# First attention: scores kept with turned sign, small norms spread between the index units, and GpSimd or VectorE scaling probabilities in place of ScalarE

## The chip, the cores and the metric

One core of a Trainium2 chip runs the whole program. The time is the device time of one execution in microseconds, lower is better; a comparison uses the median of several executions. TensorE (PE) does the matmuls and transposes, VectorE (DVE) and ScalarE (ACT) the elementwise work, GpSimd (POOL) helps with elementwise work, and SyncE (SP) issues the DMAs. Each engine runs its own instruction list in order and waits on semaphores that the others raise.

## What is computed

Two transformer blocks over 512 tokens of width 1024, all in float32. The change touches only the attention of the first block, in which two kinds of heads share one stage:

```python
def dsa_sparse_attention(q, k, v, q_idx, k_idx, w_idx):      # 8 heads, one shared key and value head
    top_k = min(TOPK_MAX, T // 4)                            # 128 of 512 keys
    def one_block(i):                                        # 128 queries
        idx_logits = jnp.einsum('bqhd,bsd->bqhs', qib, k_idx)        # 16 index heads of 64
        score = jnp.einsum('bqh,bqhs->bqs', wb, jax.nn.relu(idx_logits))
        score = jnp.where(causal[None], score, -jnp.inf)
        _, sel = lax.top_k(score, top_k)
        ...
        att = jnp.einsum('bqhd,bqkd->bqhk', qb, kg) * scale  # masked where not valid
        p = jax.nn.softmax(att, axis=-1)
        return jnp.einsum('bqhk,bqkd->bqhd', p, vg)

def mla_attention(c_q, c_kv, k_rope, g_q_lat, g_kv_lat, w_uq, w_ukv, cos_b, sin_b):   # 8 causal heads
    q = (rmsnorm(c_q, g_q_lat) @ w_uq)...                    # the small norms: 384 and 256 features
    kv = (rmsnorm(c_kv, g_kv_lat) @ w_ukv)...
    ...
        p = jax.nn.softmax(s, axis=-1)
        return jnp.einsum('bhqs,bshd->bqhd', p, v)
```

## The kernel before

The order of all work is written out by hand, engine by engine; semaphores tie the engines together. A feed-forward stage comes first, then the projections of the first block, and then the three parts that matter here.

**Index stage.** `INDEX` lists 48 index units, 16 index heads times three query tiles (query tile 0 needs no selection). For each unit PE multiplies (L874, banks 0 to 3 in turn), ACT takes the Relu into one of three slots of `SF` (L1290), and DVE adds it with its weight to the score tile in `BIAS` (L1717). The three slots mean that ACT can be at most three units ahead of DVE, and four PSUM banks that PE can be at most four ahead of ACT. Ahead of the units DVE applies the two small norms, `norm_q` in three pieces of 128x512 and `norm_kv` in two: `norm_scaled` (L1480) scales a piece into `VA`, ACT copies it rounded into `NH` (`norm_high`, L1166), and `norm_low` (L1492) keeps the rest in `NL`. The factor that they multiply by is spread over the partitions by PE (L640), after index unit 2 for `norm_q` and after unit 3 for `norm_kv`. Then DVE splits one weight tile (`split`, L1456, into `WL`), and only then takes unit 0. Units 24 to 31 of PE's list carry the values' matmuls (`values`, L843 to L845). GpSimd copies `KPE` into `KB` (L2032) as soon as the small norms are done.

**Heads.** `UNITS` lists 64 units of 128 queries: 32 of the causal heads (head by head, query tiles 0 to 3, so 128, 256, 384 and 512 keys in turn) and 32 of the sparse heads (query tile by query tile, 8 heads each). `project` (twice, ahead of units 0 and 16) makes queries and keys of four causal heads. A unit u passes through

1. PE `scores` (L929) into bank u % 2;
2. DVE `masked` (L1763): scale, add the mask, write to slot u % 4 (`VA` or, every fourth, `SA`) and take the row maximum into `NM`;
3. DVE `negated` (L1770): turn the sign of `NM`, raise `at_m`;
4. ACT `exp` (L1320) with the sum of the row into `DEN`;
5. DVE `inverse` (L1774);
6. ACT `normalised` (L1327): scale the probabilities in their slot;
7. PE `turn` (L936): one to four transposes into bank 2 + u % 2;
8. ACT `turned` (L1335): copy them to `PT`.

Each engine's loop runs over u with the steps three, two or one units ahead of the last one, and after each eight units PE multiplies with the values (`heads`, L949 for causal and L956 for sparse heads), ACT copies the result to `NH` (L1342) and DVE takes the rest (L1779). PE's list has the values' product of a group of eight behind `scores` of the unit eleven further on than the group's first, and ahead of `turn` of the next group's first unit, so everything behind it on PE waits for it. DVE also runs the selection of the 128 best keys in the gaps of its loop, one round per unit in 48 rounds: MAX8 (L1726) and MATCH_REPLACE8 (L1730), over 256 keys in the first 16 rounds, 384 in the next and 512 in the last.

In DVE's loop the order in a step u is

```python
                if 0 <= u + 1 < len(UNITS):
                    inverse(u + 1)
                ...
                if u >= 0:
                    next(selection, None)
                n = masked(u + AHEAD) if u + AHEAD < len(UNITS) else None
                if u >= 0:
                    next(selection, None)
                if n is not None:
                    negated(u + AHEAD, n)
```

**After the heads** the stages go on in a fixed order: output projection, norm, feed-forward. The next stage's first MW transfer waits for the last head's result (`at_o`), so an earlier end of the heads moves all that follows.

## Time and profile before

| | us |
|---|---|
| median of 3 runs | 2756.97 |
| lowest and highest of them | 2756.56, 2759.14 |
| the profiled execution's own time | 2751.96 |
| its span in the trace | 2750.2 |
| PE busy in it | 2669.4 (97%) |
| DVE, ACT, GpSimd busy | 1417.1 (52%), 757.8 (28%), 365.0 (13%) |

The stage of the change lies between about 541 and 777 us of the span. Times of rows are microseconds from the span's start. An instruction's duration in a row runs from its start to its result; the next instruction of the engine often starts up to 0.1 us before that end, so where instructions stand back to back the distance of starts is the price, not the duration. The end of a row in the timeline, in brackets, is the engine's idle time ahead of it and the instruction that ended it.

### The profile page before, as it was taken

How to read it: one execution, taken by the hardware profiler on the slowest of the kernel's cores; microseconds unless marked ns; L12 is line 12 of the kernel's file. 1: busy time of each engine (PE TensorE's matmuls, PEld its weight loads, DVE VectorE, ACT ScalarE, POOL GpSimd, SP SyncE). 2: the span in 40 equal slices, each digit the busy share in tenths (PEclk: the TensorE clock that was granted, in tenths of full speed). 3: DMA queues.
4: the chain of work that ended last, by engine and by line, in shares of the span. 5: the costliest groups of instructions: out<-in, count | busy, mean ns of one | idle time of the engine just before them, and what ended most of it. 6: DMA issues, size and time to landing. Idle time of an engine off the chain costs nothing.

```text
span 2750.2 us, 33754 instructions
## 1 busy us (share of the span) xinstructions
PE 2669.4 (97%) x12402; PEld 2137.0 (78%) x12402; DVE 1417.1 (52%) x2479; ACT 757.8 (28%) x1035; POOL 365.0 (13%) x274
## 2 busy tenths in 40 slices
PE   8999989988999999999999999999999999999998
PEld 6888877754467888878888888888888657888887
DVE  7777785477667666573222222354225653443334
ACT  3212123246632222241111111223222452321223
POOL 1101011000011111132202202201100003110102
PEclk9999999989799999999999999999999999999999
DMA  6444443200043445432122121222332002333331
GB/s 176 145 130 145 130 122 87 62 16 1 1 143 108 149 130 151 131 92 73 65 61 61 61 61 54 69 79 90 92 115 65 28 1 81 88 92 92 107 88 65
DMA packets 394769, 241.21 MB, mean 88 GB/s; under 512 B 14768, under 2 KB 392752, under 8 KB 394672
## 3 DMA queue, kind: packets, MB, share of 16 engines
q1 hardware_dynamic: 394672, 239.92, 29.9%
q8 instruction: 60, 0.98, 0.2%
q14 instruction: 37, 0.30, 0.0%
HBM read 237.79 MB, written 2.10 MB: 87 GB/s over the span
## 4 chain that ended last, share of the span: by engine, by line
PE 88%; DVE 6%; ACT 3%; issue 2%; DMA 1%; POOL 0%; SPq 0%; DVEq 0%; ACTq 0%; POOLq 0%
PE PS L690 22%; PE PS L692 22%; PE PS L697 22%; PE PS L672 3%; PE PS L675 3%; PE PS L673 3%; PE PS L1100 2%; PE PS L1080 1%; DVE RB L1518 1%; PE PS L874 1%; DVE WL L1456 1%; PE PS L956 1%; DVE VA L1480 1%; PE PS L949 1%; PE PS L929 1%
## 5 line engine op out<-in xcount | busy, mean ns | idle before, releaser
L690 PE MATMUL PS<-NH,WH 128*128 128x512 f32 (+1 forms) x2128 | 625.7, 375 | 10.3 <-DVE WL L1456 6.1
L692 PE MATMUL PS<-NH,WL 128*128 128x512 f32 (+1 forms) x2128 | 620.3, 373 | 0.0
L697 PE MATMUL PS<-NL,WH 128*128 128x512 f32 (+1 forms) x2128 | 591.5, 372 | 0.0
L1456 DVE TENSOR_TENSOR WL<-RAW,WH 128x2048 fp32r<-128x2048 f32 x190 | 463.4, 2439 | 102.8 <-ACT WH L1128 102.4
L1128 ACT ACTIVATE WH<-RAW 128x2048 fp32r<-128x2048 f32 x190 | 363.6, 1914 | 536.1 <-PE PS L697 505.9
L697 PEld LDWEIGHTS PS<-NL,WH 128*128 128x128 f32 x2128 | 389.7, 189 | 72.0
L692 PEld LDWEIGHTS PS<-NH,WL 128*128 128x128 f32 x2128 | 389.2, 189 | 72.1
L690 PEld LDWEIGHTS PS<-NH,WH 128*128 128x128 f32 x2128 | 383.8, 189 | 79.0 <-issue 9.2
L1518 DVE SCALAR_TENSOR_TENSOR RB<-MW,CV,RB 128x128 f32<-128x128 f32 x826 | 329.9, 432 | 17.8
L690 PE MATMUL PS<-HH,WH 128*128 128x512 f32 (+1 forms) x820 | 241.4, 375 | 1.4 <-DVE WL L1456 1.4
L1202 ACT ACTIVATE SA<-PS 128x512 f32<-128x512 f32 x104 | 62.0, 596 | 655.8 <-PE PS L697 622.5
L692 PE MATMUL PS<-HH,WL 128*128 128x512 f32 (+1 forms) x820 | 239.6, 373 | 0.0
L1975 POOL CAST HH<-VA 128x512 f32 (+2 forms) x88 | 60.5, 688 | 1291.5 <-DVE VA L1587 1291.5
L697 PE MATMUL PS<-HL,WH 128*128 128x512 f32 (+1 forms) x820 | 226.2, 373 | 0.0
L1587 DVE TENSOR_TENSOR VA<-SA,PS 128x512 f32<-128x512 f32 x88 | 60.4, 686 | 241.1 <-ACT SA L1202 241.1
L692 PEld LDWEIGHTS PS<-HH,WL 128*128 128x128 f32 x820 | 148.7, 188 | 30.0
L697 PEld LDWEIGHTS PS<-HL,WH 128*128 128x128 f32 x820 | 148.5, 188 | 30.1
L690 PEld LDWEIGHTS PS<-HH,WH 128*128 128x128 f32 x820 | 146.7, 188 | 29.8 <-DVE WL L1456 1.6
L1977 POOL TENSOR_TENSOR HL<-VA,HH 128x512 f32 (+2 forms) x88 | 167.6, 1904 | 14.2 <-POOL HH L1975 14.0
L1586 DVE TENSOR_TENSOR VA<-SA,PS 128x256 f32<-128x256 f32 x22 | 9.3, 421 | 262.5 <-ACT SA L1202 262.5
L672 PE MATMUL PS<-NH,WH 128*128 128x512 f32 x320 | 127.2, 397 | 0.0
L673 PE MATMUL PS<-NL,WH 128*128 128x512 f32 x320 | 122.3, 384 | 0.0
(298 smaller groups left out, 2630.7 us busy)
## 6 DMA issues: line engine op xcount, KB each, us to landing
RAW<-in_ffn_w_in SPq DMA_DIRECT2D x88, 512.0 KB, 4.9
MW<-in_w_mod SPq DMA_DIRECT2D x72, 512.0 KB, 3.8
RAW<-in_w_in SPq DMA_DIRECT2D x70, 512.0 KB, 4.2
RAW<-in_w_gate SPq DMA_DIRECT2D x44, 512.0 KB, 4.3
RAW<-in_w_up SPq DMA_DIRECT2D x44, 512.0 KB, 5.5
RAW<-in_w_down SPq DMA_DIRECT2D x32, 512.0 KB, 4.5
RAW<-in_ffn_w_out SPq DMA_DIRECT2D x32, 512.0 KB, 4.2
RAW<-in_w_out SPq DMA_DIRECT2D x16, 512.0 KB, 4.4
```

Source lines behind the costliest of these rows:

```text
L672: pe.matmul(o, wh, xh(k), start=k == 0, stop=False)
L673: pe.matmul(o, wh, xl(k), start=False, stop=False)
L675: last = pe.matmul(o, wl, xh(k), start=False, stop=k == kn - 1)
L690: pe.matmul(outs[half][x], w[half][0], xh(k), start=k == 0, stop=False)
L692: pe.matmul(outs[half][x], w[half][1], xh(k), start=False, stop=False)
L697: last = pe.matmul(outs[half][x], w[half][0], xl(k), start=False, stop=k == kn - 1)
L1128: act.activation(WH[1 - s][:, :], RAW[1 - s][:, :], ACT.Copy).then_inc(w_hi, 1)
L1202: act.activation(SA[:, s, 0:T], G[s][:, :], func).then_inc(gate_done, 1)
L1456: dve.tensor_tensor(WL[1 - s][:, :], RAW[1 - s][:, :], WH[1 - s][:, :].bitcast(F32), ALU.subtract).then_inc(w_lo, 1)
L1518: last = dve.scalar_tensor_tensor(out=o, in0=MW[t][:, k, :], scalar=CV2[:, k, v:v + 1], in1=o, op0=ALU.mult, op1=ALU.add)
L1975: pool.tensor_copy(h, VA[:, s, 0:tok]).then_inc(pool_s, 1)
L1977: pool.tensor_tensor(l, VA[:, s, 0:tok], h.bitcast(F32), ALU.subtract).then_inc(h_split, 1)
```

## The change

Four edits, all in the first attention.

- `masked` scales by a negative factor and takes the row minimum, so `NM` comes out with the sign that `exp` needs; `negated` is gone, `at_m` is raised by `masked` itself, and `exp` multiplies its input by -1.
- The scaling of the probabilities (`normalised`) is done by GpSimd for units 0 to 31 (semaphore `at_p`), by ACT as before for units 32 to 47, and by DVE for units 48 to 63, behind its reciprocal (`at_q`).
- The small norms are no longer ahead of the index units: piece i is scaled in front of index unit 2 + 2i on DVE, its rounded copy stands behind ACT's Relu of that unit, and its low part is in front of unit 4 + 2i.
- The weight split that stood ahead of index unit 0 stands on ACT behind unit 12 and on DVE in front of unit 14.

```diff
--- before.py
+++ after.py
@@ -189,6 +189,7 @@
         at_s, at_m, at_e, at_r, at_t, at_c = (sem(f"at_{c}") for c in "smertc")
 
         at_v, at_h, at_o, at_d = sem("at_v"), sem("at_h"), sem("at_o"), sem("at_d")
+        at_q, at_p = sem("at_q"), sem("at_p")
         conv_s = sem("conv_s")
         y_split, y_part = sem("y_split"), sem("y_part")
         ga_done = sem("ga_done")
@@ -385,7 +386,9 @@
 
         INDEX = [(q, h) for h in range(IDX_HEADS) for q in range(1, NT)]
         IX_V = 24
+        IX_NORM = 2
         AHEAD = 3
+        BY_POOL, BY_ACT = 32, 48
         def p_slot(u):
             return (VF[:, (u % 4) * T:(u % 4 + 1) * T] if u % 4 < 3 else SF[:, 2 * T:3 * T])
 
@@ -396,6 +399,10 @@
             return t[:, u % 4:u % 4 + 1]
 
         norm1 = Norm(x_src, KD, T, lambda k: vec("g_ffn1", k), n_dst, rows=True)
+
+        def small_norms(i):
+
+            return (norm_q, i, i + 1) if i < 3 else (norm_kv, i - 3, i - 2)
 
         def pj_bank(i):
 
@@ -929,7 +936,12 @@
                 pe.matmul(B[u % 2][:, 0:keys], q, k, start=True, stop=True).then_inc(at_s, 1)
 
             def turn(u):
-                pe.wait_ge(at_r, u + 1)
+                if u < BY_POOL:
+                    pe.wait_ge(at_p, u + 1)
+                elif u < BY_ACT:
+                    pe.wait_ge(at_r, u + 1 - BY_POOL)
+                else:
+                    pe.wait_ge(at_q, u + 1 - BY_ACT)
                 if u >= 2:
                     pe.wait_ge(at_c, u - 1)
                 for t in range(UNITS[u][2] + 1):
@@ -1282,16 +1294,17 @@
             norm_squares(norm_kv, 1, 2)
             norm_root(norm_q)
             norm_root(norm_kv)
-            split(v_b % 2, loaded(v_b, 1), v_b)
             for n, (q, h) in enumerate(INDEX):
                 act.wait_ge(ix_mm, n + 1)
                 if n >= 3:
                     act.wait_ge(ix_acc, n - 2)
                 act.activation(SF[:, (n % 3) * T:(n % 3) * T + (q + 1) * P], B[n % 4][:, 0:(q + 1) * P], ACT.Relu)\
                     .then_inc(ix_relu, 1)
-                if n == 2:
-                    norm_high(norm_q)
-                    norm_high(norm_kv)
+                i = (n - IX_NORM) // 2
+                if n >= IX_NORM and n % 2 == 0 and i < 5:
+                    norm_high(*small_norms(i))
+                elif n == IX_NORM + 10:
+                    split(v_b % 2, loaded(v_b, 1), v_b)
                 elif n == IX_V:
                     act.wait_ge(v_zero, 1)
                 if n >= IX_V + 2 and n % 2 == 0 and n < IX_V + 2 + 2 * NT:
@@ -1317,7 +1330,7 @@
                 act.wait_ge(at_m, u + 1)
                 keys = (UNITS[u][2] + 1) * P
                 p = p_slot(u)[:, 0:keys]
-                act.activation(p, p, ACT.Exp, bias=stat(NM, u), accum_out=stat(DEN, u))\
+                act.activation(p, p, ACT.Exp, bias=stat(NM, u), scale=-1.0, accum_out=stat(DEN, u))\
                     .then_inc(at_e, 1)
 
             def normalised(u):
@@ -1346,7 +1359,7 @@
                     project((u + AHEAD) // 16)
                 if 0 <= u + AHEAD - 1 < len(UNITS):
                     exp(u + AHEAD - 1)
-                if 0 <= u + 1 < len(UNITS):
+                if BY_POOL <= u + 1 < BY_ACT:
                     normalised(u + 1)
                 if u >= 0:
                     if u % PER_GROUP == 0 and u:
@@ -1704,11 +1717,17 @@
                     dve.wait_ge(rope_out, i + 1)
             norm_inverse(norm_q)
             norm_inverse(norm_kv)
-            norm_apply(norm_q)
-            dve.wait_ge(norm_lo, norm_q.lo + 3)
-            norm_apply(norm_kv)
-            split(v_b % 2, v_b)
             for n, (q, h) in enumerate(INDEX):
+                i = (n - IX_NORM) // 2
+                if n >= IX_NORM and n % 2 == 0 and i < 6:
+                    if i:
+                        norm_low(*small_norms(i - 1)[0:2])
+                    if i == 3:
+                        dve.wait_ge(norm_lo, norm_q.lo + 3)
+                    if i < 5:
+                        norm_scaled(*small_norms(i)[0:2])
+                elif n == IX_NORM + 12:
+                    split(v_b % 2, v_b)
                 keys = (q + 1) * P
                 acc = BIAS[:, q - 1, 0:keys]
                 dve.wait_ge(ix_relu, n + 1)
@@ -1760,18 +1779,18 @@
                     dve.wait_ge(at_t, u - 3)
                 bias = CM[:, (NT - 1 - q) * P:T] if kind == "b" or q == 0 else BIAS[:, q - 1, 0:keys]
                 scale = float(96 if kind == "b" else 64) ** -0.5
-                own.inc(dve.tensor_tensor_reduce(out=p_slot(u)[:, 0:keys], in0=B[u % 2][:, 0:keys], in1=bias,
-                                                 scale=scale, scalar=3 * NEG * 1e7, op0=ALU.add, op1=ALU.max,
-                                                 accum_out=stat(NM, u)))
-                return own.n
-
-            def negated(u, n):
-                dve.wait_ge(dve_s, n)
-                dve.tensor_scalar(stat(NM, u), stat(NM, u), -1.0, None, ALU.mult).then_inc(at_m, 1)
+                dve.tensor_tensor_reduce(out=p_slot(u)[:, 0:keys], in0=B[u % 2][:, 0:keys], in1=bias,
+                                         scale=-scale, scalar=-3 * NEG * 1e7, op0=ALU.add, op1=ALU.min,
+                                         accum_out=stat(NM, u)).then_inc(at_m, 1)
 
             def inverse(u):
                 dve.wait_ge(at_e, u + 1)
-                dve.reciprocal(stat(DEN, u), stat(DEN, u)).then_inc(at_d, 1)
+                if u < BY_ACT:
+                    dve.reciprocal(stat(DEN, u), stat(DEN, u)).then_inc(at_d, 1)
+                else:
+                    p = p_slot(u)[:, 0:(UNITS[u][2] + 1) * P]
+                    own.settle(dve, dve.reciprocal(stat(DEN, u), stat(DEN, u)))
+                    dve.tensor_scalar(p, p, stat(DEN, u), None, ALU.mult).then_inc(at_q, 1)
 
             def heads(g):
                 dve.wait_ge(at_h, g + 1)
@@ -1792,12 +1811,10 @@
                         pass
                 if u >= 0:
                     next(selection, None)
-                n = masked(u + AHEAD) if u + AHEAD < len(UNITS) else None
+                if u + AHEAD < len(UNITS):
+                    masked(u + AHEAD)
                 if u >= 0:
                     next(selection, None)
-                if n is not None:
-                    negated(u + AHEAD, n)
-                if u >= 0:
                     if u % PER_GROUP == 1 and u > 1:
                         heads(u // PER_GROUP - 1)
             heads(NG - 1)
@@ -2031,6 +2048,10 @@
             for i in range(4):
                 pool.tensor_copy(KB[64:96, i, :], KPE[64:96, :]).then_inc(kb_copied, 1)
                 pool.wait_ge(kb_copied, i + 1)
+            for u in range(BY_POOL):
+                pool.wait_ge(at_d, u + 1)
+                p = p_slot(u)[:, 0:(UNITS[u][2] + 1) * P]
+                pool.tensor_scalar(p, p, stat(DEN, u), None, ALU.mult).then_inc(at_p, 1)
             norm(norm2)
             lows(norm2)
             ffn(ffn2, T, H0["ffn2"])
```

What stands on the engines, at the places that the prediction speaks of. DVE from the end of the norm factors to the index units: L1480 and L1492 (L1493 and L1505 after) are a piece's scaling and its low part, L1456 (L1469) the weight split, L1717 (L1736) the index units. Before:

```order
L1470 TENSOR_SCALAR TA<-ident,RT 128x128 x4
L1480 SCALAR_TENSOR_TENSOR VA<-CQ,vecs,PS 128x512 x2
L1492 TENSOR_TENSOR NL<-VA,NH 128x512
L1480 SCALAR_TENSOR_TENSOR VA<-CQ,vecs,PS 128x512
L1492 TENSOR_TENSOR NL<-VA,NH 128x512 x2
L1480 SCALAR_TENSOR_TENSOR VA<-CQ,vecs,PS 128x512 x2
L1492 TENSOR_TENSOR NL<-VA,NH 128x512 x2
L1456 TENSOR_TENSOR WL<-RAW,WH 128x2048
L1717 SCALAR_TENSOR_TENSOR BIAS<-SA,WI,CM 128x256
```

After:

```order
L1483 TENSOR_SCALAR TA<-ident,RT 128x128 x4
L1736 SCALAR_TENSOR_TENSOR BIAS<-SA,WI,CM 128x256
L1736 SCALAR_TENSOR_TENSOR BIAS<-SA,WI,CM 128x384
L1493 SCALAR_TENSOR_TENSOR VA<-CQ,vecs,PS 128x512
L1736 SCALAR_TENSOR_TENSOR BIAS<-SA,WI,CM 128x512
L1736 SCALAR_TENSOR_TENSOR BIAS<-SA,WI,BIAS 128x256
L1505 TENSOR_TENSOR NL<-VA,NH 128x512
L1493 SCALAR_TENSOR_TENSOR VA<-CQ,vecs,PS 128x512
L1736 SCALAR_TENSOR_TENSOR BIAS<-SA,WI,BIAS 128x384
L1736 SCALAR_TENSOR_TENSOR BIAS<-SA,WI,BIAS 128x512
```

Five pieces that stood in one block now alternate with pairs of index units, two of which stand ahead of all of them.

ACT at the first group's values' product: L1320 (L1333) is `exp`, L1327 `normalised`, L1335 (L1348) `turned`, L1342 (L1355) the copy of the group's result. Before:

```order
L1320 ACTIVATE VA,DEN<-VA,NM 128x256
L1327 ACTIVATE VA<-VA,DEN 128x128
L1335 ACTIVATE PT<-PS 128x4x128
L1320 ACTIVATE VA,DEN<-VA,NM 128x384
L1327 ACTIVATE VA<-VA,DEN 128x256
L1342 ACTIVATE NH<-PS 128x512
```

After:

```order
L1333 ACTIVATE VA,DEN<-VA,NM 128x256
L1348 ACTIVATE PT<-PS 128x4x128
L1333 ACTIVATE VA,DEN<-VA,NM 128x384
L1355 ACTIVATE NH<-PS 128x512
L1348 ACTIVATE PT<-PS 128x128
```

One of three instructions per unit is gone from ACT. GpSimd, from its copies into `KB` on; before:

```order
L2032 COPY KB<-KPE 32x512 x4
L2008 TENSOR_TENSOR VA<-VA,SA 128x512 x6
```

After, with the first five of 32 scalings:

```order
L2049 COPY KB<-KPE 32x512 x4
L2054 ISA
L2054 TENSOR_SCALAR VA<-VA,DEN 128x128
L2054 TENSOR_SCALAR VA<-VA,DEN 128x256
L2054 TENSOR_SCALAR VA<-VA,DEN 128x384
L2054 TENSOR_SCALAR SA<-SA,DEN 128x512
L2054 TENSOR_SCALAR VA<-VA,DEN 128x128
```

The scalings stand where GpSimd had nothing to do, each behind a wait on DVE's reciprocal.

## Rows read from the trace of the kernel before

**Rows 1.** The page's first part: busy time, share of the span and instructions of each engine.

```profile
PE 2669.4 (97%) x12402; PEld 2137.0 (78%) x12402; DVE 1417.1 (52%) x2479; ACT 757.8 (28%) x1035; POOL 365.0 (13%) x274
```

**Rows 2.** Stretches: from:to, length, busy of PE, PEld, DVE, ACT, POOL, granted clock.

```profile
546.00:562.00 16.00, 12.36 (x30) 6.78 (x29) 10.89 (x18) 6.40 (x10) 2.90 (x2) 0.50 0.00 1
562.00:574.50 12.50, 11.76 (x36) 7.73 (x36) 11.43 (x20) 8.68 (x20) 2.17 (x3) 0.73 0.25 85
574.50:587.50 13.00, 13.00 (x49) 7.03 (x46) 6.67 (x12) 6.79 (x18) 0.00 (x0) 1.00 0.00 0
712.00:748.00 36.00, 35.97 (x84) 14.88 (x84) 23.98 (x96) 24.06 (x67) 0.00 (x0) 0.67 0.00 1
```

**Rows 3.** Timeline of DVE and ACT at the small norms.

```profile
551.96 1.41 DVE L1480 SCALAR_TENSOR_TENSOR VA<-CQ,vecs,PS 128x512 f32<-128x512 f32 x2 [4.75 <-PE PS L640]
552.74 1.29 ACT L1166 ACTIVATE NH<-VA 128x512 fp32r<-128x512 f32 x2 [2.19 <-DVE VA L1480]
558.89 2.28 DVE L1456 TENSOR_TENSOR WL<-RAW,WH 128x2048 fp32r<-128x2048 f32 x1
561.09 2.73 DVE L1717 SCALAR_TENSOR_TENSOR BIAS<-SA,WI,CM 128x256 f32<-128x256 f32 x3
```

**Rows 4.** One round of four causal units: all engines, then ACT's L1327 alone.

```profile
621.81:627.20 5.39, 3.92 (x19) 2.19 (x20) 5.23 (x29) 5.39 (x18) 0.00 (x0) 1.00 0.00 0
621.81:627.20 5.39, 2.21 (x4) 1.00 0.00 0
```

**Rows 5.** Timeline of DVE in that round.

```profile
623.95 0.41 DVE L1726 MAX8 M<-BIAS 128x8 f32<-128x256 f32 x1
624.52 0.69 DVE L1763 CUSTOM_DVE_ANT_0 SA<-PS,CM 128x512 f32<-128x512 f32 x1 [0.16 <-PE PS L929]
625.66 0.42 DVE L1726 MAX8 M<-BIAS 128x8 f32<-128x256 f32 x1
625.99 0.27 DVE L1763 CUSTOM_DVE_ANT_0 VA<-PS,CM 128x128 f32<-128x128 f32 x1
```

**Rows 6.** Timeline of DVE at the third group's values' product.

```profile
676.63 0.15 DVE L1774 RECIPROCAL DEN<-DEN 128x1 f32<-128x1 f32 x1
684.65 0.29 DVE L1763 CUSTOM_DVE_ANT_0 VA<-PS,CM 128x128 f32<-128x128 f32 x1 [2.62 <-PE PS L929]
```

**Rows 7.** The chain that ended last, there: start, us, what.

```profile
677.40 0.61 ACT SA L1327
679.17 0.49 ACT PT L1335
679.70 4.58 PE PS L949 x16
```

**Rows 8.** Groups of GpSimd's instructions: xcount, busy, mean ns, idle before.

```profile
L1975 POOL CAST HH<-VA 128x512 f32 x64 | 39.2, 612 | 871.9 <-DVE VA L1587 871.9
L1977 POOL TENSOR_TENSOR HL<-VA,HH 128x512 f32 x64 | 85.8, 1341 | 10.4 <-POOL HH L1975 10.4
```

**Rows 9.** L2041: duration ns min/median/max, first and last start.

```profile
L2041 POOL TENSOR_SCALAR FD<-ident,RF x4: 599/702/1078, 1232.4 to 1234.7; 128x128 f32<-128x128 f32 x4
L2041 POOLq MODIFY_POOL_CONFIG  x2: 12/12/12, 1221.2 to 1221.3; - x2
```

**Rows 10.** Timeline of GpSimd and DVE side by side in the last feed-forward stage.

```profile
2672.14 1.29 POOL L1977 TENSOR_TENSOR HL<-VA,HH 128x512 f32 x1 [0.16 <-POOL HH L1975]
2672.22 3.36 DVE L1456 TENSOR_TENSOR WL<-RAW,WH 128x2048 fp32r<-128x2048 f32 x1 [1.02 <-ACT WH L1128]
```

**Rows 11.** Timeline of DVE and PE at the last sparse units.

```profile
731.78 0.41 DVE L1734 TENSOR_SCALAR BIAS<-BIAS 128x512 f32<-128x512 f32 x1
761.39 0.66 PE L936 MATMUL PS<-ident,VA 128*128 128x128 f32 x4
761.50 0.69 DVE L1763 CUSTOM_DVE_ANT_0 SA<-PS,BIAS 128x512 f32<-128x512 f32 x1 [0.68 <-PE PS L929]
767.16 8.54 PE L956 MATMUL PS<-PT,VAP 128*128 128x512 f32 x16 [0.69 <-ACT PT L1335]
```

## The prediction, written before the result

> **What bounds the kernel now.** Read the page first: PE is busy 97% of the span, DVE 52% and ACT 28% [rows 1]. Over the whole kernel only PE matters, so a change on the other engines can pay only in stretches where PE waits or works on little. The stage of the change is such a place. The stretches show three regimes [rows 2]. From 546 to 562 us the granted clock is 0.50 (the lower level, 1.2 GHz) and DVE is busy 10.89 of 16.00: the small norms. From 574.5 to 587.5 PE is busy 13.00 of 13.00 at 1.00 (2.4 GHz): index units with the values' matmuls, PE is the bound. From 712 to 748 PE is busy 35.97 of 36.00 at a mean of 0.67: sparse units at the lower clock for much of the time, PE is the bound again. Between these lie the causal units, where in one round of four ACT is busy 5.39 of 5.39 us and DVE 5.23 [rows 4]: ACT is the bound with DVE right behind it. The timeline confirms it: DVE waits 0.16 us for scores in the round [rows 5], then runs.
>
> The second thing to see is the values' product. The third group's starts at 679.70 when ACT has made its last copy, at 679.17 [rows 7]; behind it on PE stand the scores that DVE wants, and DVE idles 2.62 us until 684.65 [rows 6]. DVE's own order is fixed, so what shortens a group is an earlier start of this product.
>
> **The change part by part.** The profiled execution took 2751.96 us with a span of 2750.2, five us under the runs' median of 2756.97. I work out differences in the trace and apply them to the median.
>
> Index stage. Units 0 and 1 now fall into the 4.75 us in which DVE waited for PE's spread factor [rows 3], and save their places later, about 1.1 us. Against that stand the five rounds of piece and unit pair. Before, the block from 551.96 to 561.09 took 9.1 us with the split of 2.28, so 6.9 for five pieces, since two scalings go ahead of the first low part. Now each round is one chain through two engines: scaling 0.70, ACT's copy 0.64 (1.29 for two), the Relu of the next unit about 0.5, its add about 0.6, the low part 0.7, and handovers, 3.3 us in all. Five rounds from 551.96 end at 568.5, a last pair takes 1.1 and the split 2.3: unit 14 starts at about 572. Before, unit 0 starts at 561.09 and DVE does 20 instructions up to 574.5 [rows 2, 3], so unit 14 starts near 571. GpSimd's four copies run beside the index adds in both kernels. I take +0.5 us, from -2.3 (the clock rises during the rounds, see the rivals) to +4.
>
> Causal rounds. Taking the scaling off ACT removes 2.21 us busy in a round [rows 4], 1.8 in steps, as each instruction runs about 0.1 us into the next. ACT falls to 3.6 and DVE binds with 5.39 less its waits: 0.16 shown as idle, and MAX8 to the masked op takes 0.57 where it is 0.33 when nothing is awaited (623.95 to 624.52 against 625.66 to 625.99) [rows 5]. About 5.1 us of work, so 0.3 us a round, in the four rounds of units 0 to 15: -1.2. From unit 16 on the selection is over 384 keys, a round of DVE is an estimate of 6 us from the 256-key steps, already above ACT's 5.39, and a round gains nothing.
>
> The negation. It is one more 128x1 instruction beside the reciprocal (0.15 us [rows 6]). On DVE I give its removal nothing: the MAX8 that follows waits for the preceding MATCH_REPLACE8 anyway. What it brings is that `at_m` comes ahead of that MATCH_REPLACE8 and not behind it, some 0.5 us earlier, for PE's scores and ACT's exp. In units 32 to 47, where ACT's scaling stays, I count -0.5.
>
> The values' products. Before, the reciprocal of the group's last unit starts at 676.63, ACT scales it only from 677.40 because exp and copies stand in front, and the product starts at 679.70 [rows 6, 7]: 3.07 us. After: reciprocal 0.15, GpSimd's scaling s of 512 keys, four transposes 0.66 [rows 11], ACT's copy 0.6 by its place in the chain [rows 7], and 0.25 for handovers: 1.66 + s. For s the trace has no row. GpSimd's one TENSOR_SCALAR took 0.60 us at its shortest over 128 elements [rows 9]; a cast of 512 takes 0.61, a two-input op of 512 takes 1.29 when undisturbed [rows 8, 10]. So s lies between 0.6 (all of the 0.60 is fixed cost) and 2.4 (all of it goes with length); I take 1.15, nearest to the two-input row. The path is then 2.8, 0.27 us shorter, and exp and the scores before it also move forward with `at_m`; I take 0.5 for each of the four causal groups, -2.0. With s = 0.6 it would be 0.55 more for each, -2.2; with s = 2.4 it is 1.25 less for each, and a round of GpSimd (0.6, 1.2, 1.8, 2.4) would be 6.0 us and replace ACT as the bound: 0.9 a round over what I count, +8.6 in all.
>
> The Trainium skill (GPSIMD Engine Reference, section 3.1) gives 1.8 cycles an element for a tight one-input loop, 769 ns for 512 elements. No row here has this form at 512; by that figure the sum would be 1.5 us lower.
>
> Sparse units 48 to 63. DVE takes over the scaling; its TENSOR_SCALAR of 512 takes 0.41 us [rows 11], and with reciprocal, masked op and settling wait a unit of DVE is 1.3 us, under PE's. From 712 to 748 PE binds [rows 2], so little moves; the seventh group's product waits for ACT's last copy like the others, -0.5. The end is where it pays: PE runs back to back up to 761.39, and then needs until 767.16 to turn three more units, because exp, scaling and copy of each queue on ACT [rows 11]. The last masked op starts at 761.50. After: 0.7 for it, exp and its sum 0.9, reciprocal and scaling 0.6, transposes 0.66, copy 0.6 and handovers 0.2 end at 765.2 and not 767.16: -2.0. Everything behind moves along, since the next stage starts on `at_o`.
>
> Sum: +0.5 - 1.2 - 0.5 - 2.0 - 0.5 - 2.0 = -5.7 us. 2756.97 - 5.7 = 2751.3 us.
>
> **The rivals.**
>
> Slow GpSimd: s of 1.8 or more. For it: 0.60 us for only 128 elements is as much as a cast of four times that [rows 8, 9]. Against: the cast and the two-input op show that GpSimd's cost does not all go with length. At 1.8 the products give back 2.6, at 2.4 the sum is -5.7 + 8.6 = +2.9: 2754 to 2760. Chance 0.13.
>
> GpSimd holds up DVE. In the trace DVE's split takes 3.36 us when GpSimd's op of 1.29 began just before it, against 2.28 alone [rows 3, 10]: the one waited for the other. If the masked op or the selection is held in the same way, each of some 28 DVE-bound units loses about half of a GpSimd op, 0.5 us, +14 us: 2765. It decides from 0.2 us a unit on (5.7 / 28). Against it: the split reads two SBUF tensors, the masked op scores from PSUM and one SBUF tensor, the selection one. Chance 0.09. The Trainium skill (SBUF — State Buffer, "SBUF: two separate sides") says that only DVE ops with two SBUF inputs or in a two-port mode contend with GpSimd; rows 10 agree, and by that rule this rival does not come.
>
> The clock. It is 0.50 until 562 and back at 1.00 by 574.5, ahead of the stretch in which PE binds [rows 2]. PE now gets its units in rounds of 3.3 us with gaps. If it stays at half through 6 us of that stretch, it costs some 3 us: 2754. If it comes back during the rounds the stage is 2.3 us shorter: 2749. The sparse stretch, mean 0.67, can shift by as much. Chance 0.15, of both kinds.
>
> Code loading. The queue shows MODIFY_POOL_CONFIG 11.2 us ahead of the first TENSOR_SCALAR [rows 9]; in the changed order an extra instruction stands between the copies and the scalings, 40 us ahead of their first use. If a load is paid at the first scaling instead, DVE and PE stand still for up to 11 us: 2757 to 2762. Chance 0.03. The Trainium skill (GPSIMD Engine Reference, section 2.1) puts such a load at about 6 us, which would give 2757.
>
> Only the tail pays: DVE and the product's handover bind in the causal heads as before. +0.5 - 0.5 - 2.0: 2755. Chance 0.12. The forecast has the remaining 0.48.
>
> **How the numbers follow.** A measurement of this kernel tells 0.2% (5.5 us) from no change. The forecast lies at that edge: its own range is 2748 to 2754, a little over half of its 0.48 is faster. Of the clock half, and of a short s, more goes to faster: 0.46. Slower than 2762.5 takes contention (0.09), the worst of the load and of slow GpSimd with a late clock (0.05): 0.14. Same has 0.40. The range goes from s = 0.6 with an early clock (-5.7 - 2.2 - 2.3 = 2746.8) to slow GpSimd with a late clock: 2746 to 2761.
>
> **What will show it.** Index: DVE's first unit near 547, unit 14 near 572, last near 596. Causal rounds of 256-key selection 5.1 us, ACT busy 3.6 in them. GpSimd's scaling of 512 keys 1.15 us; the masked ops 0.29 to 0.69 as before. DVE's idle in front of the fifth unit behind a product start 2.1 us instead of 2.62. From the last masked op to the last product 3.7 us, not 5.7. The forecast is wrong if s is above 1.6, if MAX8 or the masked op is longer beside GpSimd, or if the low clock reaches into the values' matmuls.

## The result: 0.2% slower, and what the trace after shows

The changed kernel took 2762.22 us in the median of twelve executions (2751.32 to 2767.38), the kernel before 2756.72 (2752.62 to 2760.51). The ratio is 1.0019, with a 95% interval of 1.001 to 1.0028: 5.2 us slower, and outside my range. It also scatters over 16 us, twice as wide as before. The profiled execution took 2759.00 us with a span of 2757.2, so it is 7.0 us longer than the one of before.

The page of the changed kernel, busy time by engine (answers to [rows 1]): ACT gave work away and POOL took it.

```profile
PE 2677.0 (97%) x12402; PEld 2140.8 (78%) x12402; DVE 1418.0 (51%) x2431; ACT 737.4 (27%) x987; POOL 405.0 (15%) x306
```

The stage now starts 2.7 us earlier (the factor's root on ACT is at 540.87, before at 543.61), so its parts are best compared by length. I cut it at four instructions that both kernels have: the root on ACT, DVE's weight split for `project`, ACT's fourth copy of a values' product (end of the causal groups), and DVE's last low part. In the table they are "index", "causal" and "sparse", each read off the timelines. The effect column is the measured ratio less one, times 2756; each ratio is to the kernel before in the same measurement, whose median was 2755.15 to 2755.71 in the runs e1 to e18. The column differs by up to 2.6 us from the difference of the medians (e14: -2.3 by the medians, e3: -8.9, e8: -11.4).

| kernel | index | causal | sparse | effect on the whole, us (95%) |
|---|---|---|---|---|
| before | 53.82 | 104.18 | 74.76 | |
| changed | 62.92 | 108.49 | 70.71 | +5.2 (2.8 to 7.7) |
| e1 norms and split moved, heads as before | 63.06 | 104.76 | 74.85 | +7.2 (4.4 to 10.2) |
| e12 norms moved, split stays | 54.05 | 104.21 | 74.81 | +1.7 (-1.4 to 5.0) |
| e6 split moved alone | 56.53 | 107.40 | 74.10 | +2.5 (0.0 to 5.0) |
| e2 change without norms and split | 54.96 | 107.79 | 68.86 | -8.0 (-10.7 to -5.0) |
| e10 the same again | 53.78 | 104.70 | 70.67 | -3.9 (-6.3 to -1.4) |
| e3 as e2, ScalarE for GpSimd | 53.82 | 100.44 | 67.96 | -11.0 (-14.9 to -7.2) |
| e8 as e3, GpSimd for short units | 53.53 | 100.27 | 68.84 | -9.9 (-13.2 to -6.6) |
| e15 as e2, half the columns | 53.80 | 102.97 | 68.80 | -9.1 (-12.1 to -6.3) |
| e7 sign alone | 53.78 | 100.44 | 71.55 | -5.0 (-7.4 to -2.5) |
| e4 GpSimd alone | 53.76 | 107.13 | 74.89 | +2.8 (0.3 to 5.2) |
| e11 change without GpSimd | 59.98 | 101.09 | 68.05 | -3.0 (-5.5 to -0.3) |
| e9 the changed kernel again | 63.06 | 108.24 | 67.87 | +2.5 (-0.8 to 6.1) |
| e14 change, split stays | 53.11 | 105.25 | 67.88 | +0.3 (-3.6 to 3.9) |
| e18 the same again | 54.17 | 106.28 | 68.88 | -4.1 (-7.2 to -1.4) |
| e5 as e1, units 4 to 23 twice | 62.07 | 105.72 | 74.29 | +9.4 (5.8 to 13.2) |
| e13 as e1, unit 18 twice | 62.83 | 107.22 | 74.12 | +8.0 (4.7 to 11.3) |
| e16 as e1, units 4 to 11 twice | 63.17 | 104.75 | 74.81 | +10.2 (6.6 to 13.8) |
| e17 as e1, units 12 to 23 twice | 58.86 | 104.77 | 74.87 | +4.4 (1.9 to 6.9) |

So in these two traces the change lost 9.1 us in the index stage and 4.3 in the causal heads, and won 4.1 in the sparse ones. One part of one trace carries some 3 us of scatter: with the heads as before, the causal part is 104.2 to 104.8 in five traces, but 105.7, 107.2 and 107.4 in e5, e13 and e6. Where the 9.1 went is in the stretches (answers to [rows 2]; columns as there). Ahead of 562 the mean clock is 0.61 and was 0.50: it is up for some 3 us from 555 and falls again. From 562 to 587.5 the granted clock is 0.50 and 0.57 (the 1.2 GHz level) where it was 0.73 and 1.00, and the values' matmuls of units 24 to 31 run in the 13 us from 574.5 on: 27 matmuls there, before 49, both with PE busy 13.00 of 13.00.

```profile
546.00:562.00 16.00, 13.57 (x39) 7.76 (x37) 9.32 (x15) 5.88 (x12) 0.00 (x0) 0.61 0.01 2
562.00:574.50 12.50, 11.56 (x19) 5.80 (x20) 10.84 (x16) 7.50 (x16) 4.78 (x4) 0.50 0.14 46
574.50:587.50 13.00, 13.00 (x27) 6.53 (x26) 4.81 (x9) 3.81 (x11) 0.00 (x0) 0.57 0.10 36
587.50:603.80 16.30, 16.17 (x63) 9.37 (x63) 11.31 (x22) 12.39 (x27) 0.00 (x0) 1.00 0.01 2
```

What stands in front of this in the program is the moved split. The timeline of the changed kernel shows ACT's copy of it (1.91 us), then DVE's part (2.69, beside GpSimd's copies; 2.28 in [rows 3]), then unit 14 at 571.17. I had forecast 572 in the times of the trace before, which is 28.4 us behind the root; it is 30.3 behind it here and was 27.4 (571.03). ACT's Relus wait 3.14 us for DVE, PE waits 0.50 for ACT, and the first of the values' matmuls takes 0.79 us:

```profile
565.47 1.91 ACT L1140 ACTIVATE WH<-RAW 128x2048 fp32r<-128x2048 f32 x1
568.56 2.69 DVE L1469 TENSOR_TENSOR WL<-RAW,WH 128x2048 fp32r<-128x2048 f32 x1
571.17 4.66 DVE L1736 SCALAR_TENSOR_TENSOR BIAS<-SA,WI,BIAS 128x512 f32<-128x512 f32 x8
572.36 1.41 ACT L1301 ACTIVATE SA<-PS 128x512 f32<-128x512 f32 x3 [3.14 <-DVE BIAS L1736]
573.01 4.20 PE L881 MATMUL PS<-KI,QI 64*128 64x256 f32 x8 [0.50 <-ACT SA L1301]
577.14 0.79 PE L850 MATMUL PS<-WH,NH 128*128 128x512 f32 x1
```

In the causal heads GpSimd's scaling is at fault. Its rows by form (32 units; busy, mean ns) settle the price that no row of before had:

```profile
L2054 POOL TENSOR_SCALAR SA<-SA,DEN 128x512 f32<-128x512 f32 x8 | 12.5, 1563 | 32.0 <-DVE DEN L1789 31.9
L2054 POOL TENSOR_SCALAR VA<-VA,DEN 128x384 f32<-128x384 f32 x8 | 9.9, 1243 | 9.5 <-DVE DEN L1789 9.5
L2054 POOL TENSOR_SCALAR VA<-VA,DEN 128x256 f32<-128x256 f32 x8 | 7.4, 926 | 5.9 <-DVE DEN L1789 5.9
L2054 POOL TENSOR_SCALAR VA<-VA,DEN 128x128 f32<-128x128 f32 x8 | 4.8, 603 | 51.4 <-DVE DEN L1789 51.4
```

It is 1.56 us for 512 keys, where I took 1.15. The third group's product (answers to [rows 6, 7]) starts 4.25 us behind the last reciprocal, before 3.07. The transposes wait for POOL and take 0.88 where they took 0.66, as the clock falls to 0.50 at 688.2:

```profile
686.05 0.16 DVE L1789 RECIPROCAL DEN<-DEN 128x1 f32<-128x1 f32 x1
686.30 1.56 POOL L2054 TENSOR_SCALAR SA<-SA,DEN 128x512 f32<-128x512 f32 x1
687.91 0.88 PE L948 MATMUL PS<-ident,SA 128*128 128x128 f32 x4 [0.46 <-POOL SA L2054]
688.84 0.60 ACT L1348 ACTIVATE PT<-PS 128x512 f32<-128x512 f32 x1 [1.01 <-PE PS L948]
690.30 5.14 PE L961 MATMUL PS<-PT,VB 128*128 128x512 f32 x16
695.80 0.29 DVE L1782 CUSTOM_DVE_ANT_0 VA<-PS,CM 128x128 f32<-128x128 f32 x1 [3.44 <-PE PS L936]
```

At the end of the heads (answers to [rows 11]) the last masked op to the last product is 4.00 us, before 5.66; I had forecast 3.7. The whole last group, from ACT's seventh copy to its eighth, is 3.07 us shorter (764.78 to 782.36, before 755.09 to 775.74).

```profile
771.19 0.69 DVE L1782 CUSTOM_DVE_ANT_0 SA<-PS,BIAS 128x512 f32<-128x512 f32 x1 [0.34 <-PE PS L936]
775.19 1.98 PE L968 MATMUL PS<-PT,VAP 128*128 128x512 f32 x4 [0.69 <-ACT PT L1348]
```

### The profile page after: what moved, and what is told of

Same layout as the page of the kernel before. It is cut to its first block, busy times and chain, and to the rows that moved or that the text cites. A ratio compares the mean times of both kernels' runs of the same rounds, so it can differ in the third digit from the quotient of the medians.

```text
span 2757.2 us, 33690 instructions
## 1 busy us (share of the span) xinstructions
PE 2677.0 (97%) x12402; PEld 2140.8 (78%) x12402; DVE 1418.0 (51%) x2431; ACT 737.4 (27%) x987; POOL 405.0 (15%) x306
## 4 chain that ended last, share of the span: by engine, by line
PE 89%; DVE 6%; issue 2%; ACT 1%; POOL 1%; DMA 0%; DVEq 0%; SPq 0%; ACTq 0%; POOLq 0%
PE PS L697 22%; PE PS L699 22%; PE PS L704 22%; PE PS L682 3%; PE PS L679 3%; PE PS L680 3%; PE PS L1112 2%; PE PS L936 1%; DVE RB L1531 1%; PE PS L1092 1%; PE PS L881 1%; DVE WL L1469 1%; PE PS L968 1%; PE PS L636 1%; PE PS L948 1%
## 5 line engine op out<-in xcount | busy, mean ns | idle before, releaser
L1469 DVE TENSOR_TENSOR WL<-RAW,WH 128x2048 fp32r<-128x2048 f32 x190 | 460.9, 2426 | 101.7 <-ACT WH L1140 101.1
L1994 POOL TENSOR_TENSOR HL<-VA,HH 128x512 f32 (+2 forms) x88 | 173.3, 1970 | 14.7 <-POOL HH L1992 14.5
```

Of the source, the lines that this page charges most:

```text
L1469: dve.tensor_tensor(WL[1 - s][:, :], RAW[1 - s][:, :], WH[1 - s][:, :].bitcast(F32), ALU.subtract).then_inc(w_lo, 1)
L1994: pool.tensor_tensor(l, VA[:, s, 0:tok], h.bitcast(F32), ALU.subtract).then_inc(h_split, 1)
```

## The experiments

**e1, norms and split alone.** The two edits of the index stage on the kernel before:

```diff
-            norm_apply(norm_q)
-            dve.wait_ge(norm_lo, norm_q.lo + 3)
-            norm_apply(norm_kv)
-            split(v_b % 2, v_b)
+                if n >= IX_NORM and n % 2 == 0 and i < 6:   # pieces of the norms
...
+                elif n == IX_NORM + 12:
+                    split(v_b % 2, v_b)
```

> The kernel before with one part of the change: the small norms' pieces stand between the index units and the weight split stands at units 12 and 14; scores, negation and scaling are as before. Theory 1 (the clock): in the changed kernel PE gets its index units in rounds with gaps, the granted clock stays at 0.50 up to about 586 us and the values' matmuls run at half speed; between the factor's root and the first matmuls of project the changed kernel took 9 us more. This part alone should then be 6 to 9 us slower than before (2763 to 2766), with a granted clock near 0.5 in the stretch of index units 16 to 31. Theory 2 (GpSimd's scaling is what costs): this part gives my old sum of +0.5 us, 2757, and the clock is 1.00 ahead of the values.

Measured +7.2. Index 63.06 as in the changed kernel, clock at 0.50 from 564 to 591, causal and sparse within 0.6 of before. The loss of the index stage stands alone.

**e2 and e10, all but that.** The changed kernel with norms and split in their block (the `-` and `+` of e1 exchanged), twice.

> The changed kernel with the small norms and the weight split put back in their block ahead of index unit 0; sign, GpSimd scaling of units 0 to 31 and DVE scaling of units 48 to 63 stay. Theory 1: what is left loses some 4 us in the causal heads (first product 15.5 us behind the first masked op and not 14.5) and gains some 4 in the sparse heads, so -3 to +1 against before (2754 to 2758), clearly faster than the changed kernel. Theory 2: the loss is in the heads, so it is as slow as the changed kernel, +5 (2762).

> The run with the norms in their block once more, for a second trace: the first profiled execution was the slowest of its seven (2756.7, the others 2747 to 2751) and showed the clock at 0.50 in four stretches of the causal heads. If such dips are chance and cost those 6 us, this trace has fewer of them and its own time lies near 2750.

-8.0 and -3.9, beyond my expectation in the first. The first trace was of the slowest of its seven executions and its clock is low from 663 to 666, 680 to 683 and 697 to 703; the second (its time 2751.11) has it low from 680 to 684 and 697 to 701 only, and is 3.1 us shorter in the causal part. So short falls of the clock between groups come and go with the execution, and must be part of the scatter.

**e3, e4, e7: the heads' edits apart.** e3 is e2 with one line, e7 takes the sign alone, e4 GpSimd alone (the other edits left out).

```diff
-        BY_POOL, BY_ACT = 32, 48
+        BY_POOL, BY_ACT = 0, 48
```

> As the run with the norms in their block, but ScalarE scales the probabilities of units 0 to 31 again, as before (no GpSimd in the heads). Left of the change are the turned sign and DVE's scaling of units 48 to 63. Both theories: the sparse gain of 3 to 5 us stays and the causal loss goes, -3 to -5 against before (2752 to 2754), so 3 to 5 us faster than the run with GpSimd in it. If GpSimd's scaling is harmless in itself, the two runs are equal within 1 us.

> The kernel before with one part of the change: GpSimd and not ScalarE scales the probabilities of units 0 to 31; the negation stays, ScalarE scales units 32 to 63, norms as before. The GpSimd op took 0.60, 0.92, 1.24 and 1.56 us for 128 to 512 keys in the changed kernel. Theory 2 and theory 1 in its part on the heads: 3 to 5 us slower than before (2760 to 2762), all of it ahead of unit 32. Rival (the longer path is paid back by the idle ScalarE, whose exp and copies come earlier): within 1 us of before.

> The kernel before with the turned sign alone: no negation, ScalarE scales everything. The run with sign and VectorE scaling was 11 us faster than before. My prediction gave the sign some 0.5 us. Theory 3: the earlier at_m shortens every round and the low-clock episodes between groups, so the sign alone brings 5 to 7 of the 11 us (2749 to 2751). Rival (VectorE's scaling of units 48 to 63 brings nearly all): 0 to -2 (2754 to 2756).

-11.0, +2.8 and -5.0. The sign alone shortens the causal part by 3.7 and the sparse one by 3.2 us; DVE's scaling of units 48 to 63 adds 3.6 in the sparse one and nothing elsewhere; GpSimd, put on top of them (e10 and e2 against e3), lengthens the causal part by 4.3 to 7.4. That loss is larger than the scatter: the causal part is 104.7 to 108.5 in all six traces with the sign and GpSimd's full scaling, and 100.3 to 101.1 in the four where ScalarE scales the 512-key units (e3, e7, e8, e11). The 107.13 of e4, taken by itself, is within it, beside the 107.4 of e6. So are 2.3 of the 3.2 us that the sign wins in the sparse part. They lie in the sixth group, which takes 18.6 us in e7 and 20.9 before, but also 19.0 in e6 and e13, with the heads as before, and 21.0 in the changed kernel and e10, with the sign; around it the clock is low for 20 to 24 us in some traces and for 31 in others. In the kernel with the sign alone the third product is 2.61 us behind the reciprocal (3.07 before) and DVE waits 2.10 us behind it, with ACT scaling as ever: ACT's order is the same, but since `at_m` no longer waits for MATCH_REPLACE8 and the negation, exp and with it the scaling start earlier. The exp of the group's last unit, first before, then in e7:

```profile
675.42 0.72 ACT L1320 ACTIVATE SA<-SA,NM 128x512 f32<-128x512 f32 x1 [0.48 <-DVE NM L1770]
674.85 0.72 ACT L1320 ACTIVATE SA<-SA,NM 128x512 f32<-128x512 f32 x1
```

The scaling and the product of e7:

```profile
676.58 0.15 DVE L1769 RECIPROCAL DEN<-DEN 128x1 f32<-128x1 f32 x1
676.77 0.72 ACT L1327 ACTIVATE SA<-SA,DEN 128x512 f32<-128x512 f32 x1
679.19 4.58 PE L949 MATMUL PS<-PT,VB 128*128 128x512 f32 x16
684.14 0.29 DVE L1763 CUSTOM_DVE_ANT_0 VA<-PS,CM 128x128 f32<-128x128 f32 x1 [2.10 <-PE PS L929]
```

**e8 and e15: is it GpSimd's length or the handover?** e8 gives GpSimd the 128-key and 256-key units alone; e15 halves the columns of its op and leaves the other half unscaled, so its output is not right and only its time is of use. (The remarks behind # in the diffs are added; in e8 the waits of PE and ACT follow the edit.)

```diff
+                if u % 4 >= 2:      # e8: these stay with ScalarE
+                    continue
...
-                p = p_slot(u)[:, 0:(UNITS[u][2] + 1) * P]
+                p = p_slot(u)[:, 0:(UNITS[u][2] + 1) * P // 2]      # e15
```

> The run with sign and VectorE scaling, in which GpSimd scales the 128-key and 256-key units of 0 to 31 (0.60 and 0.92 us in the changed kernel) and ScalarE the 384-key and 512-key ones. The last unit of a group of eight has 512 keys, so the handover to the product is again ScalarE's. If GpSimd's length at 512 keys is what costs the 3 us between the runs with and without GpSimd, this is as fast as without it or up to 3 us faster, 2744 to 2747; if any wait on GpSimd costs, it is 1 to 2 us slower, 2748.

> The run with the norms in their block (sign, GpSimd, VectorE), in which GpSimd scales only the first half of each unit's columns; the other half goes unscaled into the product, so the output is not the reference's. Its op should take 0.44, 0.60, 0.76 and 0.92 us in place of 0.60 to 1.56. If the length of GpSimd's op is what costs, this is as fast as the run with ScalarE scaling, -10 to -12 against before (2744 to 2746); if handing over to GpSimd costs whatever the length, it stays at -4 to -8 (2748 to 2752).

Causal 100.27 in e8, as without GpSimd, and 102.97 in e15, between the 100.44 without it and 104.70 to 108.49 with it. The whole is at -9.9 and -9.1. So handing the short units to GpSimd, off the path to the product, costs nothing that can be measured, and the length of the op on that path costs most of the rest. Some 2.5 us of causal part remain in e15; its op of 0.92 us is still longer than ACT's 0.72, and its clock falls at 618 and 676, where that of e3 does not, so this trace leaves open whether the handover on the path has a price of its own. e15's forms (192 columns are half of 384):

```profile
L2047 POOL TENSOR_SCALAR SA<-SA,DEN 128x256 f32<-128x256 f32 x8 | 7.4, 922 | 33.4 <-DVE DEN L1782 33.4
L2047 POOL TENSOR_SCALAR VA<-VA,DEN 128x192 f32<-128x192 f32 x8 | 6.1, 762 | 9.3 <-DVE DEN L1782 9.3
```

**e6 and e12: norms or split?** e6 is before with the split alone moved, e12 is e1 with the split back ahead of unit 0.

> The kernel before with the weight split alone moved from ahead of index unit 0 to behind unit 12 (ScalarE) and ahead of unit 14 (VectorE); the small norms stay in their block. PE's gap while VectorE works at norms is 2.3 us shorter, but a new one of about 2.3 us opens at unit 14. Clock theory: a new gap behind the rise of the clock can bring it down again, 0 to +4 against before. Rival (only the spread-out norms starve PE): within 1 us of before, 2755 to 2757, and the clock is back at 1.00 by 570 us.

> The run with the norms alone, but the weight split stays ahead of index unit 0 on both engines. The split's move alone was +2 to +3 us, norms and split together +7. If the two add up, the norms' interleaving alone is +4 to +5 (2760) with the clock back by about 580 us; if the clock stays at 0.50 as long as with the moved split (about 586 us), +6 to +8 (2762).

Alone, the split's move costs 2.7 us of index (clock up at 570, down again from 577 to 580) and the norms 0.2 (clock up at 572); the 9.2 of both are no sum. The rival in e6's expectation, that only the spread-out norms matter, does not fit the index stage (the whole, +2.5 with 0.0 to 5.0, would not tell). A part of the interaction is plain. Before, the split stood on DVE between the norms and unit 0. With the norms spread, as in e12, the same place lies in DVE's wait for PE's spread factor: the split runs at 547.24, the wait ahead of the first scaling is 0.83 us where it is 2.57 in e1, and unit 14 comes 26.7 us behind the root and not 30.3. So 3.7 of e1's 9.0 us over e12 are lost ahead of unit 14, and 5.3 behind it. First e12, two rows, then e1:

```profile
547.24 2.29 DVE L1461 TENSOR_TENSOR WL<-RAW,WH 128x2048 fp32r<-128x2048 f32 x1 [0.71 <-ACT WH L1133]
551.28 0.75 DVE L1485 SCALAR_TENSOR_TENSOR VA<-CQ,vecs,PS 128x512 f32<-128x512 f32 x1 [0.83 <-PE PS L645]
554.84 0.75 DVE L1486 SCALAR_TENSOR_TENSOR VA<-CQ,vecs,PS 128x512 f32<-128x512 f32 x1 [2.57 <-PE PS L645]
```

And the clock. e12 and e1 side by side; e1 comes to the stage 3.0 us later, so its stretches are 3 us later. First e12:

```profile
568.00:572.00 4.00, 4.00 (x12) 2.30 (x10) 4.00 (x7) 1.89 (x4) 3.07 (x4) 0.50 0.00 0
572.00:576.00 4.00, 4.00 (x16) 2.38 (x14) 4.00 (x8) 3.19 (x8) 0.20 (x1) 1.00 0.00 0
584.00:588.00 4.00, 4.00 (x17) 2.00 (x15) 2.36 (x4) 2.63 (x9) 0.00 (x0) 1.00 0.00 0
```

Then e1:

```profile
571.00:575.00 4.00, 4.00 (x10) 2.51 (x9) 3.30 (x5) 3.36 (x5) 2.71 (x4) 0.50 0.00 0
575.00:579.00 4.00, 3.50 (x7) 1.23 (x5) 4.00 (x5) 1.25 (x3) 2.06 (x1) 0.50 0.22 67
587.00:591.00 4.00, 4.00 (x8) 1.94 (x7) 1.37 (x2) 1.64 (x4) 0.00 (x0) 0.50 0.00 0
```

In the first stretch both show PE busy 4.00 of 4.00 at 0.50, with 12 and 10 matmuls. In the second e12 is at 1.00 and e1, in which PE idles 0.50 us at the moved split, at 0.50.

**e5, e13, e16, e17: more matmuls for PE.** Each is e1 with index products computed twice, units 4 to 23, 18, 4 to 11 and 12 to 23.

```diff
+                if 12 <= n < IX_V:      # e17; e5: 4 <= n < IX_V; e16: 4 <= n < 12; e13: n == 18
+                    pe.matmul(B[n % 4][:, 0:(q + 1) * P], QI[r, h // 2, q * P:(q + 1) * P], KI[r, 0:(q + 1) * P],
+                              start=True, stop=True)
```

> The run with the norms alone, in which PE computes each index product of units 4 to 23 twice, the second over the first, so that the extra matmuls fill part of PE's gaps and the results stay the same. The run with the norms alone was 7 to 8 us slower than before, with a granted clock of 0.50 from 562 to 590 us, through the whole stretch of the values' matmuls. If the thin feed of PE keeps the clock down, it now rises earlier, within some 6 us after the rounds start, and at least half of those 8 us come back (2756 to 2760). Rival: the rounds themselves and the longer handovers cost the time and the clock only goes with it; then twice the matmuls can only add, 2764 or more.

> The run with the norms and the split's move alone, in which PE computes the index product of unit 18 twice. PE's gap of 0.50 us at 577.85, while VectorE splits the weights ahead of unit 14, is then filled and nothing else is added. Clock theory in its sharp form: this one gap keeps the clock at 0.50 for the next 12 us; without it the clock is back at 1.00 by some 578 us, and 4 to 6 of the 9 us of the index stage come back (+1 to +4 against before, 2757 to 2760). Rival: the gap is only a sign of thin work all along; the clock still rises at about 590 and the run is at +7 (2763) like the one without the extra product.

> The run with the norms and the split's move alone, in which PE computes each index product of units 4 to 11 twice, those that fall into the rounds with the norms. Filling one gap at the split (unit 18 twice) changed nothing, filling all of units 4 to 23 brought the clock to 1.00 at 563 us and kept it there. If it is the thin feed in the rounds that counts, the clock is up by about 565 us and stays up through the values, and the index stage is 3 to 5 us shorter than with the norms alone (total +3 to +5 against before). If the stretch behind the rounds counts, it stays or falls back to 0.50 and the run is at +8 or more.

> The same with units 12 to 23 computed twice, the stretch from the split to the values. PE is already busy there nearly without a gap at half clock, so if the feed in the rounds decides, the clock still rises only at 586 to 590 us or later and the doubled products add their own time, +12 or more against before. If the stretch behind the rounds decides, the clock is up before 580 us and the run is at or below the +7 of the norms alone.

In e5 the clock is at 1.00 from 563 on, through all of the values, with PE busy 18.40 of 20 us:

```profile
568.00:588.00 20.00, 18.40 (x64) 10.01 (x62) 16.01 (x24) 9.94 (x21) 4.78 (x4) 1.00 0.15 52
```

From the split's start to `project`'s the kernel takes 31.2 us where e1 takes 35.4; but the doubled products make the rounds 3.2 us longer, and the whole is +9.4, a miss in time. e13 is a miss altogether: PE has no gap from 566.1 to 589.2 and the clock stays at 0.50 until 589, so the theory of the one gap fell:

```profile
566.10:589.20 23.10, 23.10 (x41) 12.09 (x42) 15.13 (x22) 10.34 (x21) 4.78 (x4) 0.50 0.13 45
```

The end of a matmul is modelled in these profiles, so PE can stand as busy while it is held up. e16 and e17 then tell where it counts. In e16, with the rounds filled, the clock is up at 563, falls again at 570, where the doubling has ended and PE idles 0.67 and 0.99 us between units, and stays down through the split until 587:

```profile
570.00:586.00 16.00, 15.50 (x28) 7.60 (x28) 13.22 (x20) 8.41 (x16) 4.78 (x4) 0.50 0.20 66
```

In e17 it is up at 570 and stays up; with twice the products of twelve units it is still 4.2 us shorter in the index stage than e1. Of the two outcomes named for e17 it is the second, the stretch behind the rounds (+12 or more was the first), and e16 at +10.2 fits it. In the whole, e17 (+4.4) and e1 (+7.2) have intervals that overlap; the 4.2 us are from one trace each. e17's stretches:

```profile
564.00:568.00 4.00, 3.79 (x8) 2.47 (x10) 3.16 (x6) 2.57 (x6) 0.00 (x0) 0.50 0.00 0
568.00:572.00 4.00, 4.00 (x18) 2.99 (x18) 3.29 (x4) 2.79 (x5) 3.29 (x4) 0.75 0.00 0
572.00:576.00 4.00, 4.00 (x16) 2.35 (x13) 4.00 (x7) 1.65 (x4) 1.49 (x1) 1.00 0.37 122
```

And e13's, 2 us later, as its stage is:

```profile
570.00:574.00 4.00, 4.00 (x10) 2.53 (x9) 3.30 (x4) 2.63 (x5) 3.44 (x4) 0.50 0.00 0
574.00:578.00 4.00, 4.00 (x7) 1.96 (x7) 4.00 (x7) 1.80 (x4) 1.34 (x1) 0.50 0.41 139
```

**e9, e11, e14, e18: do the parts add up?** e9 is the changed kernel, e11 has `BY_POOL` 0 in it, e14 and e18 are the changed kernel with only the split back ahead of unit 0.

> The changed kernel itself once more, beside the next three on one chip. It was 5 us slower than before; the norms alone were 7 slower and all the rest 8 faster, which adds to -1. If the parts add up and the first figure was scatter between chips, it comes out within 2 us of before. If they do not add up, it is again 4 to 6 us slower, and the clock dips of the causal heads stand in its trace again.

> The changed kernel with ScalarE in place of GpSimd for the scaling of units 0 to 31: norms between the index units, turned sign, VectorE's scaling of 48 to 63. Sum of the parts: -11 for sign and VectorE, +7 for the norms, -4 against before (2752). If it is at -4, all that keeps the changed kernel from being faster besides the norms is GpSimd; if it is 0 or above, the norms do more harm in company than alone.

> The changed kernel with one thing undone: the weight split is ahead of index unit 0 again on both engines; norms between the index units, sign, GpSimd and VectorE scaling stay. Norms alone without the split's move were +1 in the run, all of the heads' change -4 to -8. If the parts add up: -3 to -7 (2749 to 2753), so the split's move is what turned the change into a loss. Rival (norms and heads' change disturb each other): 0 or above.

> The changed kernel with the weight split ahead of unit 0 once more. Its twelve times fell into two groups, eight near 2750 (2747 to 2754) and four near 2763 (2760 to 2766), and its trace is of the fastest (index stage +53.1 us behind the root, clock up by 573 us). If the index stage's clock is what separates the groups, a trace of a slow execution shows the index stage near +62 us with 0.50 up to about 588, and one of a fast execution shows +53 to +54 again; a slow one with +54 would put the difference elsewhere.

The changed kernel again: +2.5, index 63.06. Over both its runs it is near +4; e14 and e18, +0.3 and -4.1, are near -2. That is 6 us for the split's place in the changed kernel. The intervals of the two pairs only just part, and e14's alone overlaps with both of the changed kernel's. e11 is at -3.0, against the sum of -4 (its clock is up at 582 and its index 59.98); it differs from the changed kernel in GpSimd's scaling alone, so that costs 5.5 to 8.2 us of the whole there. Parts add up within the scatter. The times of e14 fell into two groups (2747 to 2754, and four of 2760 to 2766). The traces of e14 and e18 are both of the lower group, index 53.11 and 54.17, so what the upper one is stays open; a late clock in the index stage would have its size, but no slow execution of either was traced.

The fastest right kernels are e3 and e8, with the norms and split where they were: -11.0 and -9.9, medians 2746.73 and 2743.75.

## Why the prediction was wrong

In terms of the sum, I had the causal part at -3.2 (-1.2 and -2.0) and the sparse one at -3.0; the traces have +4.3 and -4.1. With the index stage at +9.1 for +0.5, two steps failed, by 8.6 and 7.5 us.

**The index stage** is the first step that failed. I put it at +0.5, and gave the clock's rival 6 us of the values' stretch at half speed, +3. It was +9.1. That unit 14 stands at 571.17 and the forecast said 572 is luck: this execution came to the stage 2.7 us earlier. Behind the root, unit 14 is 2.9 us later than before, 1.9 more than forecast: the split took 2.69 for 2.3, and the last pair ahead of it waited for ACT, which was at its own part of the split. Unit 14 to `project`'s split then took 32.6 us (571.17 to 603.79), and 26.4 before (571.03 to 597.43), 6.2 more. By e5 and e17, at least 4.2 us of that is the clock; the other 2 are not separated. I had looked at the norms' rounds as the danger, had named the low clock there as a rival at +3, and had moved the split as if it were free there. e12 shows the norms nearly free as long as the split fills DVE's wait, e1 that the split behind them is not: for 1.91 us on ACT and 2.69 on DVE it holds up the Relus just ahead of the stretch in which PE binds, where before PE had a wait of 4.38 us around it:

```profile
562.74 12.06 PE L874 MATMUL PS<-KI,QI 64*128 64x384 f32 x36 [4.38 <-ACT SA L1290]
```

**GpSimd's scaling** is the second, a mis-sized term. The path was right: 1.66 + s, with s = 1.56, is 3.22 us, and e14's third product, at full clock, starts 3.22 behind its reciprocal:

```profile
677.95 0.15 DVE L1787 RECIPROCAL DEN<-DEN 128x1 f32<-128x1 f32 x1
678.20 1.56 POOL L2052 TENSOR_SCALAR SA<-SA,DEN 128x512 f32<-128x512 f32 x1
681.17 4.57 PE L961 MATMUL PS<-PT,VB 128*128 128x512 f32 x16
```

So s was above the two-input row (1.29), and I had taken it below: by my own sum this is 0.41 us in each group, 1.6 in all. I also compared with 3.07, which is not what ScalarE needs: once the sign is turned it needs 2.61. Against that, GpSimd loses 0.6 us in the second and third group, some 0.1 in the first and 1 in the fourth, and more where the clock then falls (4.25 in the changed kernel). In the causal part it costs 4.3 us (e10 against e3) to 7.4 (the changed kernel against e11), and the 3.2 that I had hoped to gain there never came. DVE's idle time of 2.1 us behind the product, forecast for the changed kernel, came in e7; in the changed kernel it is 3.44.

**The negation** was the opposite: I gave it -0.5 and it brings -5.0. The mechanism that I named, `at_m` ahead of MATCH_REPLACE8, was right, but I priced it in units 32 to 47 and at some 0.2 us in each causal product. It shortens each of the first six groups, by 1.8, 0.4, 0.6, 0.9, 0.9 and 2.3 us, in part because the clock fell less: before it was low from 616 to 620 and from 705 to 736, with the sign alone from 704 to 714 and 721 to 731. The last 2.3 are the sixth group, whose clock varies with the execution, so it carries some 4.7 of the traces' 7 us without that; the runs say 5.0 (2.5 to 7.4).

**The causal rounds.** I had ACT as their bound, and that was wrong. Units 4 to 7 take 5.38 us before and 5.09 in e7, the forecast 5.1, with ACT scaling as ever: what bound them went through the negation, and taking scalings off ACT as well gave next to nothing (5.04 in e8 and e15). With GpSimd they take 5.66 (e2, e9, e10, e14, e18), and 6.78 in the changed kernel, where the clock is at 0.50 from 626.8 to 630.2. ACT's share fell there to 4.03 of 6.80 us, and DVE waits for scores, 0.90 us before one unit, that stand on PE behind a transpose waiting for GpSimd. DVE's own ops were not held up: the masked op takes 0.27 to 0.69 as before, and MAX8 0.43, as in e3 and e7, where GpSimd does nothing in the heads (0.41 before). So that rival is out, as the rule in the Trainium skill (SBUF — State Buffer, "SBUF: two separate sides") would have it.

```profile
627.47 0.43 DVE L1745 MAX8 M<-BIAS 128x8 f32<-128x256 f32 x1
628.80 0.56 DVE L1782 CUSTOM_DVE_ANT_0 VA<-PS,CM 128x384 f32<-128x384 f32 x1 [0.90 <-PE PS L936]
```

**Seventh group and tail** held: -0.54 for -0.5, and -3.07 for -2.0 (1.7 of it in the stretch I had worked out, the rest in the units ahead, which no longer queue on ACT).

Code loading was not paid at the first scaling, which took 0.61 us like the other seven of its form. In the traces the stage is 9.1 + 4.3 - 4.1 = 9.3 us longer; less the 2.7 by which this execution came to it earlier, that is 6.6 of the 7.0 us between the spans.

## What to carry to other kernels

An edit that moves work out of a wait has to be priced where it lands: a 2 us piece that costs little in a wait ahead of a slow stretch cost 2.7 us (e6) and 9.0 (e1 against e12) just ahead of the stretch that TensorE bounds, which it then entered or ran in part at half clock. Do not take TensorE's busy share in a profile as a sign that the clock will be up: it was 23.10 of 23.10 us at 0.50 in e13 and 18.40 of 20.00 at 1.00 in e5. And take an instruction off the path before handing one to another engine: the removed sign change gave 5.0 us, the handovers to GpSimd (a loss) and VectorE (a gain of some 6, e3 against e7) together between a loss of 1 and a gain of 3 (e10 and e2 against e7). It also lowered the mark that the handover had to beat.
